# The expert rows' gather-and-add and the memory keys' scaling: from VectorE to GpSimd

## The reference, cut to what matters

```python
def moe_ffn(h, router_w, router_b, w_gate, w_up, w_down):   # 8 experts, top 2, expert width 3584
    logits = t @ router_w + router_b
    top_vals, top_idx = lax.top_k(logits, 2)
    top_w = jax.nn.softmax(top_vals, axis=-1)
    gates = jnp.sum(jax.nn.one_hot(top_idx, 8) * top_w[..., None], axis=1)
    for e in range(8):
        out = out + gates[:, e:e + 1] * swiglu(t, w_gate[e], w_up[e], w_down[e])
...
h = rmsnorm(h + moe_ffn(rmsnorm(h, g)), final_g)            # the second block's input
...
mk = rmsnorm_2(to_heads(mk, 4, 128), g_mem_k)               # memory keys, normed by head
o_mem = memory_attention(mq, mk, mv)
```

## Time and profile before

| | |
|---|---|
| median of 3 runs | 1861.65 us (1859.37 to 1862.70) |
| the profiled execution | 1863.01 us, its span 1860.9 us |
| PE busy / weight loads | 1837.7 us (99%) / 1524.2 us |
| DVE (VectorE) busy | 1430.6 us (77%) |
| ACT (ScalarE) busy | 1234.5 us (66%) |
| POOL (GpSimd) busy | 108.1 us (6%) |
| granted TensorE clock | 0.998 |

### The profile page before, as it was taken

How to read it: one execution, slowest core, us unless ns; L and a number is a source line. 1 busy time by engine, 2 the same in 40 slices (tenths; PEclk the granted TensorE clock), 3 DMA queues, 4 the chain that set the end, 5 groups by cost and what they waited for, 6 DMA issues and landing times.

```text
span 1860.9 us, 26626 instructions
## 1 busy us (share of the span) xinstructions
PE 1837.7 (99%) x9714; PEld 1524.2 (82%) x9714; DVE 1430.6 (77%) x1229; ACT 1234.5 (66%) x1107; POOL 108.1 (6%) x150
## 2 busy tenths in 40 slices
PE   9999999989999999999999999999999999999998
PEld 8888887878888888888888888888877788888887
DVE  5654657767988888989889898898997777776554
ACT  6543467465877778787787777877767468645452
POOL 0100011122200000000000000000401100000000
PEclk9999999999999999999999999999999999999999
DMA  8974544026999999999999999999995333445551
GB/s 325 388 275 152 207 156 158 26 73 237 385 417 378 386 374 400 364 375 402 359 399 372 367 402 361 397 382 365 378 381 204 146 126 114 161 178 187 192 186 68
DMA packets 76780, 521.10 MB, mean 280 GB/s; under 512 B 8224, under 2 KB 8480, under 8 KB 17568
## 3 DMA queue, kind: packets, MB, share of 16 engines
q1 hardware_dynamic: 72368, 503.27, 70.0%
q0 software_dynamic: 4192, 16.25, 2.2%
q10 hardware_dynamic: 144, 0.52, 0.1%
HBM read 501.14 MB, written 18.87 MB: 279 GB/s over the span
## 4 chain that ended last, share of the span: by engine, by line
PE 76%; DVE 3%; issue 1%; ACT 1%; POOL 0%; ACTq 0%; DVEq 0%; POOLq 0%
PE bank L937 16%; PE bank L932 16%; PE bank L933 16%; PE bank L560 7%; PE bank L567 7%; PE bank L561 7%; PE bank L954 1%; DVE w_lo L2453 1%; PE bank L632 1%; PE bank L752 1%; PE bank L609 0%; PE bank L1204 0%; DVE w_lo L2101 0%; PE bank L982 0%; PE bank L762 0%
## 5 line engine op out<-in xcount | busy, mean ns | idle before, releaser
L2453 DVE TENSOR_TENSOR w_lo<-raw,w_hi 128x2048 fp32r<-128x2048 f32 x336 | 761.9, 2289 | 102.9 <-ACT w_hi L1644 99.1
L1644 ACT ACTIVATE w_hi<-raw 128x2048 fp32r<-128x2048 f32 x336 | 643.0, 1919 | 145.2 <-PE bank L937 144.2
L2101 DVE TENSOR_TENSOR w_lo<-raw,w_hi 128x2048 fp32r<-128x2048 f32 (+2 forms) x137 | 298.1, 2183 | 127.4 <-ACT w_hi L1420 125.5
L1420 ACT ACTIVATE w_hi<-raw 128x2048 fp32r<-128x2048 f32 (+2 forms) x137 | 250.3, 1829 | 169.2 <-PE bank L567 161.2
L932 PE MATMUL bank<-w_hi,xT 128*128 128x512 f32 x896 | 353.7, 395 | 0.0
L933 PE MATMUL bank<-w_hi,xT 128*128 128x512 f32 x896 | 349.2, 390 | 0.0
L560 PE MATMUL bank<-w_hi,xT 128*128 128x512 f32 (+1 forms) x752 | 294.7, 394 | 0.2 <-DVE xT L2133 0.2
L561 PE MATMUL bank<-w_hi,xT 128*128 128x512 f32 (+1 forms) x752 | 289.1, 386 | 0.0
L937 PE MATMUL bank<-w_lo,xT 128*128 128x512 f32 x896 | 240.8, 390 | 1.3 <-DVE w_lo L2453 1.0
L937 PEld LDWEIGHTS bank<-w_lo,xT 128*128 128x128 f32 x896 | 167.6, 188 | 39.2 <-DVE w_lo L2453 4.2
L932 PEld LDWEIGHTS bank<-w_hi,xT 128*128 128x128 f32 x896 | 168.3, 188 | 34.1 <-issue 0.2
(11 more groups left out here) (476 smaller groups left out, 1835.1 us busy)
## 6 DMA issues: line engine op xcount, KB each, us to landing
raw<-in_experts_dram SPq DMA_DIRECT2D x336, 1024.0 KB, 6.9
raw<-in_tiles_dram SPq DMA_DIRECT2D x124, 1024.0 KB, 4.8
rows_in<-zeros POOLq DMA_DIRECT2D x1, 6144.0 KB, 32.4
raw<-in_tiles_dram SPq DMA_DIRECT2D x11, 512.0 KB, 4.0
rows_out<-zeros POOLq DMA_DIRECT2D x1, 5632.0 KB, 54.9
item_rows<-rows_in SPq DMA_DIRECT2D x7, 512.0 KB, 7.4
rows_out<-y_s SPq DMA_DIRECT2D x7, 512.0 KB, 3.5
row<-in_rows_dram SPq DMA_DIRECT2D x1, 1040.0 KB, 12.5
```

The source lines that it names most:

```text
L1420: nc.scalar.activation(w_hi[:, i % SPL, 0:kc * w], raw[:, i % DENSE, 0:kc * w], ACT.Copy)\
L1644: nc.scalar.activation(w_hi[:, w_slot(j), :], raw[:, raw_slot(j), :], ACT.Copy).then_inc(m_hi, 1)
L2101: nc.vector.tensor_tensor(w_lo[:, i % SPL, 0:kc * w], raw[:, i % DENSE, 0:kc * w], w_hi[:, i % SPL, 0:kc * w], ALU.subtract).then_inc(spli ...
L2453: nc.vector.tensor_tensor(w_lo[:, s, :], raw[:, raw_slot(j), :], w_hi[:, s, :], ALU.subtract).then_inc(m_lo, 1)
```

## The change

VectorE loses `head_scale("mk")`, all four `combine` calls and the `rows_read` flag. GpSimd takes them: the keys are multiplied right behind their inverse roots, ahead of the first gather, in one TENSOR_TENSOR of 128 x 1024; each `combine` becomes, for each token tile, a TENSOR_TENSOR that multiplies the rows with the gate in place and a second one that adds them to `h`, both of 128 x 512, four in all. They stand behind the gathers, `collect(1, 1)` between `combine(0, 0)` and the other three. New waits: GpSimd for `gates_ready` (set at the end of VectorE's gate weights); VectorE, ahead of `add_last(c)`, for `combined`; TensorE, ahead of the memory keys' transposes, for `k_scaled`. The counts on `h_scaled` shift by one.

```diff
@@ TensorE, second_block @@
-                    if HEADED[name][1]:
-                        pe.wait_ge(h_scaled, NORMED.index(name) + 1)
+                    if name == "mk":
+                        pe.wait_ge(k_scaled, 1)
+                    elif HEADED[name][1]:
+                        pe.wait_ge(h_scaled, NORMED.index(name))
@@ GpSimd @@
             head_root(0, "mk")
+            keys = staged("mk").rearrange("p (a b) -> p a b", b=MEM_HD)
+            n = NT * CB // MEM_HD
+            tell(nc.gpsimd.tensor_tensor(keys, keys, hs[:, 1, 0:n].unsqueeze(2).broadcast_to((P, n, MEM_HD)), ALU.mult),
+                 k_scaled)
...
+            def combine(c, k):
+                for tt in range(NT):
+                    j = TOP_K * tt + k
+                    pool.wait_ge(collected[c][j], 16)
+                    hh = h[:, tt, c * CB:c * CB + CB]
+                    rows = later_rows[c][:, tt, :] if k else xn[:, tt, c * CB:c * CB + CB]
+                    own(nc.gpsimd.tensor_tensor(rows, rows, dest_gate[:, j:j + 1].broadcast_to((P, CB)), ALU.mult))
+                    tell(nc.gpsimd.tensor_tensor(hh, hh, rows, ALU.add), combined)
+
             collect(0, 0)
             collect(0, 1)
             collect(1, 0)
-            pool.wait_ge(rows_read, 1)
+            pool.wait_ge(gates_ready, 1)
+            combine(0, 0)
             collect(1, 1)
+            combine(0, 1)
+            combine(1, 0)
+            combine(1, 1)
@@ VectorE, the last item @@
                         if final and f == 3:
-                            head_scale("mk")
                             place_last()
-                        if final and f == 4:
-                            combine(0, 0)
-                            tell(nc.vector.memset(small[:, 70:71], 0.0), rows_read)
-                        if final and f == 5:
-                            combine(0, 1)
-                        if final and f == 6:
-                            combine(1, 0)
...
                     if final:
-                        split_until(4 * FB + 4 + SPL)
-                        combine(1, 1)
                         split_until(5 * FB - 1 + SPL)
...
-            def combine(c, k):
...
-                    own(nc.vector.scalar_tensor_tensor(out=hh, in0=rows, scalar=dest_gate[:, j:j + 1], in1=hh,
-                                                       op0=ALU.mult, op1=ALU.add))
             def add_last(c):
+                dve.wait_ge(combined, 4 * (c + 1))
```

More of the change, by code:

```diff
@@ L447, in build @@
         rows_stored = sem("rows_stored")
-        rows_read = sem("rows_read")
+        gates_ready = sem("gates_ready")
+        k_scaled = sem("k_scaled")
+        combined = sem("combined")
         last_placed = sem("last_placed")
@@ L2487, in gate_weights @@
                     own(nc.vector.tensor_tensor(mine, mine, gate.unsqueeze(2).broadcast_to(both_k), ALU.mult))
-                    own(nc.vector.tensor_reduce(dest_gate[:, :].rearrange("p (t k) -> p t k", t=NT), mine, AX, ALU.add))
+                    tell(nc.vector.tensor_reduce(dest_gate[:, :].rearrange("p (t k) -> p t k", t=NT), mine, AX, ALU.add),
+                         gates_ready)
                 last = last_item(dve)
```

## The result

The changed kernel takes **1865.47 us** (median of 20 runs, 1862.94 to 1868.11), the kernel before in the same comparison 1861.47 us (20 runs, 1859.37 to 1865.14). The ratio is 1.002, with a 95% interval of 1.0014 to 1.0026: 4.0 us slower (2.6 to 4.8). The difference lies at the bound of 0.2% that parts "within" from "slower".

What follows compares the result with a forecast made beforehand. TensorE bounds the kernel, with VectorE short of room in the last expert item. Terms +0.4, +0 and +1.9 make +2.3 us; from the median of 1861.65 that forecasts 1863.9 us, likeliest range 1860.5 to 1866.5, wider 1858.3 to 1868.8.

Steps and rivals of the forecast that it cites:

- within: Whole kernel: a change of no more than 0.2%, 3.7 us, either way; chance 0.62.
- slower: Whole kernel: slower by over 0.2%, 3.7 us; chance 0.27.
- Turns by whole instructions: Rows of `w_lo`: each GpSimd instruction of s us holds VectorE up by s - 0.20 us.
- VectorE isn't held up: Rival, last expert item: only GpSimd waits, TensorE's waits vanish, -4.3 us, 1857.4 us; chance 0.13.
- Whole spans: Rival, every `w_lo` following a GpSimd instruction: price s, not s - 0.20; +6.1 us, 1867.8 us; chance 0.25.
- the likeliest case: Last expert item: the forecast itself, +2.3 us, 1863.9 us, own range 1860.5 to 1866.5; chance 0.55.
- To product 16: Last item's start: the keys' turn costs VectorE 1.7 us in place of 1.28 us of `head_scale`; +0.4 us.
- Products 20 to 29: Last item: three `combine` go, 4.9 us; eight GpSimd instructions come, 5.3 us after cover; waits stay, +0.
- Products 30 to 41: Last item: eight GpSimd instructions make `w_lo` of product 39 3.35 us late, less 1.4 us of cover; +1.9 us.
- the cover of 1.4 us: `add_last(0)` ended at 1403.7, TensorE came to its transposes at 1405.16: lateness up to 1.4 us costs nothing.
- The new wait for half 0: Sign near the item's end: TensorE's L609 waits for `add_last(0)`, 1 to 3 us.
- the 1406 of the step: GpSimd's end in the last item: near 1406, with sixteen instructions taking up to 54 us.

Runs made afterwards that it cites:

- experiment 1: The changed kernel without GpSimd's sixteen multiplications and additions; gathers, keys and flags stay: 1858.85 us, ratio 0.9988.
- experiment 3: The changed kernel with each of GpSimd's sixteen instructions replaced by two memsets of the same rows, which only write: 1858.21 us, ratio 0.9985.
- experiment 8: The changed kernel with GpSimd's eight multiplications reading one tensor and a scalar per partition instead of two tensors: 1860.90 us, ratio 0.9996.
- experiment 11: The kernel before with one unused VectorE sum of 1.22 us ahead of `hnat` of block 6, nothing on GpSimd: 1864.01 us, ratio 1.0014.
- experiment 4: The changed kernel with VectorE's `hnat` of block 6 ahead of the `w_lo` of product 29: 1864.19 us, ratio 1.0016.
- experiment 6: The kernel before with the second half's `combine` moved late, ahead of `add_last(1)`, four instructions in effect: 1862.02 us, ratio 1.0002.
- experiment 7: The kernel before with all the `combine` and key-scaling work still on VectorE but later, nothing on GpSimd: 1857.67 us, ratio 0.9978.

## Why the prediction was right, and where its sizes were off

**The mechanism was right.** Turns by whole instructions, s - 0.20 us of held VectorE each: forecast 0.84, 1.08 and 1.7 us, measured 0.83 and 0.87 for a multiplication (`w_lo` of 3.12 and 3.16 us), 0.98 to 1.09 for an addition (3.27 to 3.38) and 1.70 us; one beside an evacuation costs 0.24 where 0.84 - 0.60 was forecast. Over the item that is 1.7 + 15.4 less 3.4 of cover = 13.7 us forecast, 13.6 measured. Experiments 1, 3 and 8 show the cause: GpSimd's operations on two tensors take the turns, its memsets take none, and its operation on one tensor nearly none. "VectorE isn't held up" is refuted by the `w_lo` of 3.12 us and more. "Whole spans" is refuted by their size: it asked for 1.04 and 1.28, and only the first multiplication cost 1.04. There the `w_lo` was shown 0.11 us ahead of GpSimd and waited; at 260.78 one shown as far ahead went first, so the shown starts don't settle who goes first. The Trainium skill ("SBUF — State Buffer", Summary: rules for kernel authors) says that the second instruction to issue is blocked until the first finishes. That holds here but for the 0.2 us; experiment 8 shows a one-tensor GpSimd instruction that reads SBUF and holds up a `w_lo` beside it by 0.4 us at most, which the rule doesn't part from the others.

Two readings of the prediction were off without consequence. The trace of before has a third meeting: at 296.11 GpSimd's next multiplication took 3.22 us behind the same `w_lo` and ended 1.15 us after it, 0.13 less than its 1.28. And the likeliest case's own range ends by its terms at 1866.9 us, not 1866.5.

**To product 16: right.** +0.4 forecast, +0.37 measured (product 16), from the keys.

**Products 20 to 29: mis-sized, the term that failed.** "About the same ... +0" was forecast; measured are +1.1 by VectorE and +1.35 by the clock. The step's own sum was 5.3 us that come against 4.9 us that go, a loss of 0.4 that I rounded to nothing. In fact nine GpSimd instructions, not eight, started ahead of `hnat` (GpSimd began 55.7 us into the item, not 57.0, and `hnat` came 1.5 us later in it than before), and the `w_lo` 20 to 29 are 5.9 us longer together: 5.9 - 4.9 = 1.0. In experiment 11 the same lateness without any GpSimd work has the same effect.

The clock was in no term. Behind 2.8 us without work TensorE ran at the lower level for 3.4 us: the transposes took 0.76 us where they took 0.41, product 29 3.85 where 2.85. It comes back in all three executions of the changed kernel and in experiment 11, and is absent in experiment 4, where the wait is gone, and in experiment 8, where it is 1.6 us. So 2.45 us were missing from this term; the total is off by only 0.9 us (2.3 against 3.2) because the next term erred the other way, and that is luck. The lateness was priced by the right mechanism; the clock's 1.35 us had no place in it.

**Products 30 to 41: too large.** +1.9 forecast, +0.35 measured (0.30 of it at product 38, L611). The step counted VectorE 3.35 us late against TensorE. It was 1.5: `add_last(0)` ended 2.79 us behind the start of product 38 (1405.30 + 1.41 against 1403.92), where it ended 1.28 behind it before (1403.71 against 1402.43). Product 38 starts with these rows, before the change and after it:

```profile
1402.43 0.39 PE L932 MATMUL bank<-w_hi,hid 128*128 128x512 f32 x1
```

```profile
1403.92 0.39 PE L934 MATMUL bank<-w_hi,hid 128*128 128x512 f32 x1
```

What was left out: seven GpSimd instructions, not eight, were left for this stretch, 0.84 us; and while TensorE ran at the lower clock it lost about 1.35 us that VectorE did not lose. Together that is 2.2 us, about the 1.85 that are missing; how it divides was not tested. Against the cover of 1.4 us that the earlier trace rows gave, 1.5 us late leaves a wait of 0.1, and 0.30 was measured. The new wait for half 0, forecast with 1 to 3 us, is 0.5 us (L611).

**The rest.** GpSimd ended at 1396.1, inside the 1395 to 1410 that was forecast but ahead of the 1406 of the step: 54 us at full waits was its upper bound. The new waits on VectorE for `combined` cost nothing, and behind the item nothing moved, both as forecast. The traces give 0.4 + 1.1 + 1.35 + 0.35 = 3.2 us; the timings give 4.0 with 3.2 inside the interval. No trace places the 0.8 us between them.

**Where the expected gain went.** Four `combine` of 1.65 us left VectorE, 6.6 us; GpSimd's sixteen turns held it up by 11.9 us (13.6 less the keys' 1.7). Without those turns 2.4 us of gain stand (experiment 1). Experiment 7 gains 4.2 of the 4.3 us of waits without a second engine, by moving the same work to where VectorE has room.

## What to carry to other kernels

An idle engine isn't free if its reads of two tensors take turns with the busy one: price a moved instruction by what it holds up, s less the handover, and compare that with its length where it was. Look first for a later place on the same engine: here the room was 27 to 74 us further on, and using it beat both kernels. A TensorE wait of some 3 us should be priced with what the clock takes behind it, from rows at the lower level (here 1.35 to 1.6 us).

## What the runs showed of the hardware that I had not expected

- The granted clock fell to 0.5 (1.2 GHz) for 3.4 us at 1375 in four of four executions in which TensorE had waited 2.8 to 3.1 us there, and in none with a wait of 1.7 us or less there; it cost 1.35 us in the changed kernel and 1.6 us in experiment 11. At 1468 a wait of 1.5 us had it fall in one profile (experiment 6, 1.4 us) and not in the others, so the length of the wait alone doesn't settle it.
- A GpSimd operation with one tensor and one scalar per partition takes hardly a turn from `w_lo`: 4.55 us for a pair beside it, and 0.4 us more at most for a single one, while it takes 4.2 us itself on the mean (33.7 us over eight).
- Memsets on GpSimd run beside `w_lo` at 0.53 us, with no delay on either side.
